# Reordering the first block's projections (values ahead of keys, low parts ahead of modulation sums) and splitting p's projection into three single-pass products

## The reference, cut to what matters

```python
x = layer_norm(x, ln_emb_g, ln_emb_b)
z = x @ w_in[i]
xs, gs, cq, ckv, kr, gm = jnp.split(z, IN_SPLIT_POINTS, axis=-1)
ys = s5_branch(xs, ...) * jax.nn.silu(gs)      # state space branch: y @ w_glu
ym = mla_branch(cq, ckv, kr, ...)              # q = norm(cq) @ w_uq, kv = norm(ckv) @ w_ukv, rotary
...
ple = jax.nn.sigmoid(u @ w_pg[i]) * (p[i] @ w_pp[i])
```

## Time and profile before

| | |
|---|---|
| median of 3 runs | 2211.8 us |
| the profiled execution | 2214.04 us, its span 2211.3 us |
| granted TensorE clock, mean | 0.986 |
| PE busy | 96% |
| DVE, POOL, ACT busy | 56%, 56%, 35% |

### The profile page before, as it was taken

One profiled execution on the slowest core, in us unless ns is written; L12 is line 12 of the kernel. 1 busy time (PEld: TensorE's weight loads), 2 busy tenths in 40 slices (PEclk: granted clock), 3 DMA queues, 4 the chain that ended last, 5 costly groups with the idle time before them and its releaser, 6 DMA issues.

```text
span 2211.3 us, 28169 instructions
## 1 busy us (share of the span) xinstructions
PE 2119.7 (96%) x11208; PEld 1653.5 (75%) x11208; DVE 1230.6 (56%) x1476; ACT 777.4 (35%) x1188; POOL 1239.1 (56%) x826
## 2 busy tenths in 40 slices
PE   8989989999998999999999999998899999999998
PEld 3878835878875885578767788786788888888886
DVE  6999836541768115510168226867766666652424
ACT  6222342340117005620174442145454554431211
POOL 1485812047873663337656754473788888844441
PEclk9999989999998999999999999999999999999999
DMA  7462460042332321001221225323122222154112
GB/s 290 141 145 94 110 214 29 1 164 95 104 100 76 120 77 46 28 29 67 55 47 58 96 108 206 122 76 126 43 82 86 86 86 86 58 191 143 48 39 76
DMA packets 66033, 212.68 MB, mean 96 GB/s; under 512 B 15159, under 2 KB 17511, under 8 KB 64719
## 3 DMA queue, kind: packets, MB, share of 16 engines
q1 hardware_dynamic: 52624, 152.73, 20.7%
q10 hardware_dynamic: 9040, 36.45, 4.5%
q0 software_dynamic: 4240, 21.70, 3.5%
HBM read 162.73 MB, written 46.17 MB: 94 GB/s over the span
## 4 chain that ended last, share of the span: by engine, by line
PE 85%; DVE 6%; ACT 3%; POOL 2%; issue 2%; DMA 1%; SPq 0%; ACTq 0%; DVEq 0%
PE ps L3304 22%; PE ps L2916 17%; PE ps L3423 11%; PE ps L2938 6%; PE ps L3228 4%; PE ps L3337 3%; PE ps L2881 3%; PE ps L3375 2%; PE ps L355 2%; PE ps L525 1%; PE ps L513 1%; PE ps L378 1%; PE ps L1036 1%; PE ps L507 1%; PE ps L538 1%
## 5 line engine op out<-in xcount | busy, mean ns | idle before, releaser
L1589 POOL TENSOR_TENSOR w_parts<-front,sb_zero 128x1024 fp32r<-128x1024 f32 x69 | 140.7, 2039 | 282.1 <-PE ps L3423 117.7
L1664 POOL TENSOR_TENSOR up_parts<-front,up_parts 128x512 fp32r<-128x512 f32 x120 | 194.5, 1628 | 70.4 <-ACT up_parts L1966 70.3
L3423 PE MATMUL ps<-ffn_parts,w_parts 128*128 128x512 f32 x1008 | 230.3, 389 | 1.5 <-DVE front L2842 1.5
L1594 POOL TENSOR_TENSOR w_parts<-front,w_parts 128x1024 fp32r<-128x1024 f32 x75 | 208.5, 2780 | 22.2 <-ACT w_parts L2121 7.5
L3423 PEld LDWEIGHTS ps<-ffn_parts,w_parts 128*128 128x128 f32 x1008 | 189.0, 188 | 41.7 <-issue 2.6
L3304 PE MATMUL ps<-t_high,up_parts 128*128 128x512 f32 x640 | 205.6, 392 | 5.8 <-ACT back L1973 4.6
L2916 PE MATMUL ps<-h_high,w_parts 128*128 128x512 f32 x672 | 187.6, 394 | 0.6 <-PE ps L3228 0.6
L1474 POOL TENSOR_TENSOR front<-front,sb_csilu 128x1024 f32<-128x1024 f32 x48 | 102.2, 2129 | 114.4 <-DMA front<-w_ada 114.4
L3304 PE MATMUL ps<-h_high,up_parts 128*128 128x512 f32 x480 | 154.6, 389 | 1.5 <-DVE back L2610 1.5
L3304 PEld LDWEIGHTS ps<-t_high,up_parts 128*128 128x128 f32 x640 | 121.4, 190 | 31.9 <-issue 6.5
L2916 PEld LDWEIGHTS ps<-h_high,w_parts 128*128 128x128 f32 x672 | 124.0, 188 | 25.8 <-issue 1.4
(11 more groups left out here) (429 smaller groups left out, 4870.8 us busy)
## 6 DMA issues: line engine op xcount, KB each, us to landing
front<-w_ada SPq DMA_DIRECT2D x48, 512.0 KB, 3.7
front<-w_up SPq DMA_DIRECT2D x44, 512.0 KB, 4.4
front<-w_down SPq DMA_DIRECT2D x22, 512.0 KB, 3.5
front<-w_in SPq DMA_DIRECT2D x16, 512.0 KB, 4.8
front<-w_out SPq DMA_DIRECT2D x16, 512.0 KB, 4.9
residual<-back ACTq DMA_DIRECT2D x2, 4096.0 KB, 15.6
front<-w_gates SPq DMA_DIRECT2D x16, 512.0 KB, 4.1
gates<-back SPq DMA_DIRECT2D x16, 512.0 KB, 3.6
```

Source lines behind the costliest of these rows:

```text
L1589: pool.tensor_tensor(high, raw, zero[:, 0:1].to_broadcast((P, PAGE)), ALU.add)\
L1594: pool.tensor_tensor(low, raw, high.bitcast(F32), ALU.subtract).then_inc(S("w_split"), 1)
L1664: pool.tensor_tensor(parts[:, BANK:], src, parts[:, 0:BANK].bitcast(F32), ALU.subtract)\
L3423: mm = pe.matmul(ps[:, 2 * m + nt, :], parts[n % 2 + w_][:, at:at + P], half_of(AR[kk % 4 + x_], nt), start=k == 0 and q == 0, stop=k == N ...
```

## The change

p's projection: p and the first weights come in halves and quarters; they are rounded (weights by ACT, p by DVE) and their low parts made (GpSimd, DVE), and each half becomes six single-pass products. Halves 0 to 7 go by token half; ten halves instead of eight stand ahead of the sums over x. DVE evacuates halves 10, 11 and 12 between centring and the reciprocal, ACT the others. GpSimd makes the low part of a tile's weights ahead of the modulation sum, and PE's column moves from k=0 to k=6 of the tile. The spread for kv moves in front of tile 15's last 16 products, the one for q behind the third round of states. The values come ahead of the keys, the keys use banks 5, 0, 2 and 5, the rotated q and the sigmoid's tiles start in banks 4 to 7. In GpSimd's queue the stores of y come first and the gates' loads last.

```diff
...
-        PP_BANK = (4, 5, 6, 7, 0, 1, 4, 5, 0, 1, 2, 0, 1, 2, 3, 2)
-
-        def pp_half(pe, s):
-
...
+        PP_HALF = [(m, nt) for nt in range(2) for m in range(4)] + [divmod(s, 2) for s in range(8, 16)]
+        PP_BANK = (4, 5, 6, 7, 0, 1, 4, 5, 6, 7, 0, 1, 2, 2, 3, 2)
...
+
...
+
+        def pp_products(pe, halves, ready=None):
+
+            for n, (w_, x_) in enumerate(((W_PP_HIGH, PT_HIGH), (W_PP_LOW, PT_HIGH), (W_PP_HIGH, PT_LOW))):
+                for s in halves:
+                    if ready:
+                        ready(n, s)
+                    m, nt = PP_HALF[s]
+                    for kt in range(2):
+                        at = kt * BANK + m % 4 * P
+                        mm = pe.matmul(ps[:, PP_BANK[s], :], w_[:, m // 4, at:at + P],
+                                       x_[:, kt, nt * BANK:(nt + 1) * BANK], start=n == 0 and kt == 0,
+                                       stop=n == 2 and kt == 1)
+                    if n == 2:
+                        mm.then_inc(S("pp_tile"), 1)
         def embed_pe(pe):
-            pe.wait_ge(S("p_landed"), 32)
...
+            def first_ready(n, s):
+
+                if s == 0 and n != 1:
+                    pe.wait_ge(S("dve_step"), DVE_STEP["p_high0" if n == 0 else "p_low0"])
+                if s in (0, 2) and n == 0:
+                    pe.wait_ge(S("act_step"), ACT_STEP["w_pp_high0"] + s // 2)
+                elif s in (0, 2) and n == 1:
+                    pe.wait_ge(S("pool_step"), POOL_STEP["w_pp_low0"] + s // 2)
+
+            pp_products(pe, (0, 1, 2, 3), first_ready)
+            pe.wait_ge(S("dve_step"), DVE_STEP["p_low1"])
+            pp_products(pe, (4, 5))
+            pe.wait_ge(S("pp_free"), 1)
+            pp_products(pe, (6, 7))
+            pe.wait_ge(S("pp_free"), 2)
+            pe.wait_ge(S("act_step"), ACT_STEP["w_pp_high2"])
+            pe.wait_ge(S("pool_step"), POOL_STEP["w_pp_low2"])
+            pp_products(pe, (8, 9))
             pe.wait_ge(S("x_added"), 1)
...
-            pe.wait_ge(S("pp_free"), 3)
+            pe.wait_ge(S("pp_free"), 5)
             pe.wait_ge(S("norm_stat_read"), 1)
...
-            pe.wait_ge(S("w_pp_landed"), 16)
-            pp_half(pe, 8)
-            pp_half(pe, 9)
+            pp_products(pe, (10, 11))
             for k in range(FT):
-                if k == 2:
-                    pp_half(pe, 10)
+                if k == 3:
+                    pp_products(pe, (12,))
                 pe.wait_ge(S("norm_square"), k + 1)
                 sum_tiles(pe, 3, ones[:], TEMPS_1[k % 2], k == 0, k == FT - 1).then_inc(S("norm_square_used"), 1)
-            pe.wait_ge(S("pp_free"), 4)
-            pp_half(pe, 11)
+            pe.wait_ge(S("pp_read_dve"), 2)
+            pp_products(pe, (13,))
             pe.wait_ge(S("norm_rstd"), 1)
             spread_tiles(pe, TEMPS_1[2][:, 256:512]).then_inc(S("norm_spread"), 1)
-            pp_half(pe, 12)
-            pe.wait_ge(S("pp_free"), 5)
-            pp_half(pe, 13)
-            pe.wait_ge(S("norm_std"), 1)
-            pp_half(pe, 14)
-            pe.wait_ge(S("pp_free"), 8)
-            pp_half(pe, 15)
+            pp_products(pe, (14,))
+            pe.wait_ge(S("pp_free"), 6)
+            pp_products(pe, (15,))
...
+            def projected(s, n=2):
+
+                m, nt = PP_HALF[s]
                 act.wait_ge(S("pp_tile"), s + n)
...
-
-            for m in range(1, 4):
-                projected(2 * m, 2, m)
...
+                if s < 8:
+                    dst, src = PP_FIRST[0][:, m:m + 2, nt * BANK:(nt + 1) * BANK], ps[:, PP_BANK[s]:PP_BANK[s] + 2, :]
+                else:
+                    dst = PP_FIRST[1][:, m % 4, nt * BANK:(nt + n) * BANK]
+                    src = ps[:, PP_BANK[s]:PP_BANK[s] + n, :].rearrange("p a b -> p (a b)")
+                act.activation(dst, src, ACT.Copy).then_inc(S("pp_free"), 1)
+
+            projected(0)
+            act.wait_ge(S("w_pp_landed"), 16)
+            act.activation(pp_piece(W_PP_HIGH, 2), pp_piece(W_PP, 2), ACT.Copy).then_inc(S("act_step"), 1)
+            projected(2)
+            projected(4)
+            projected(6)
+            act.wait_ge(S("pp_free"), 4)
             act.dma_start(pp_dram[0], PP_FIRST[0]).then_inc(S("pp_out0"), 16)
+            projected(8)
             for k in range(FT):
...
                 act.activation(TEMPS_1[k % 2], XN[:, k, :], ACT.Square).then_inc(S("norm_square"), 1)
-            projected(8, 2, 4)
...
-            projected(10, 1, 5)
             in_high(act, 0)
-            projected(11, 1, 6)
+            projected(13, 1)
             in_high(act, 1)
-            late = {0: 12, 2: 13, 3: 14, 5: 15}
             for k in range(FT):
                 act.wait_ge(S("norm_scaled"), k + 1)
                 act.activation(XH[k], XN[:, k, :], ACT.Identity, bias=V("ln_emb_b", k)).then_inc(S("norm_ready"), 1)
-                if k in late:
-                    projected(late[k], 1, 0)
-            act.wait_ge(S("pp_free"), 10)
+            projected(14, 1)
+            projected(15, 1)
+            act.wait_ge(S("pp_free"), 8)
+            act.wait_ge(S("pp_read_dve"), 2)
...
         def embed_dve(dve, link):
-            dve.wait_ge(S("pp_tile"), 2)
-            dve.tensor_copy(PP_FIRST[0][:, 0, :], two(4)).then_inc(S("pp_read_dve"), 1)
             for k in range(1, 6):
...
+            for s, n in ((10, 2), (12, 1)):
+                m, nt = PP_HALF[s]
+                dve.wait_ge(S("pp_tile"), s + n)
+                dve.tensor_copy(PP_FIRST[1][:, m % 4, nt * BANK:(nt + n) * BANK],
+                                ps[:, PP_BANK[s]:PP_BANK[s] + n, :].rearrange("p a b -> p (a b)"))\
+                    .then_inc(S("pp_read_dve"), 1)
...
+        K_BANK = (5, 0, 2, 5)
...
-            sp.dma_start(PT_FIRST, t["pT"].rearrange("(k p) t -> p k t", p=P)).then_inc(S("p_landed"), 16)
-            sp.dma_start(W_PP[:, 0, :], t["w_pp"][0]).then_inc(S("p_landed"), 16)
+            p_in = t["pT"].rearrange("(k p) t -> p k t", p=P)
+            w_pp_in = t["w_pp"][0].rearrange("p (k n) -> p k n", k=2)
+            sp.dma_start(PT_FIRST[:, :, 0:BANK], p_in[:, :, 0:BANK]).then_inc(S("p_landed"), 16)
+            sp.dma_start(pp_piece(W_PP, 0), w_pp_in[:, :, 0:256]).then_inc(S("p_landed"), 16)
+            sp.dma_start(pp_piece(W_PP, 1), w_pp_in[:, :, 256:512]).then_inc(S("p_weight_landed"), 16)
+            sp.dma_start(PT_FIRST[:, :, BANK:2 * BANK], p_in[:, :, BANK:2 * BANK]).then_inc(S("p_later_landed"), 16)
             sp.dma_start(XN[:, 0:2, :], x_in[:, 0:2, :]).then_inc(S("landed0"), 16)
             sp.dma_start(W_PP[:, 1, :], t["w_pp"][1]).then_inc(S("w_pp_landed"), 16)
...
+            for i in range(3):
+                pool.wait_ge(S("act_step"), ACT_STEP[f"w_pp_high{i}"])
+                pool.tensor_tensor(pp_piece(W_PP_LOW, i), pp_piece(W_PP, i), pp_piece(W_PP_HIGH, i).bitcast(F32),
+                                   ALU.subtract).then_inc(S("pool_step"), 1)
...
             for i in range(6, N_IN):
-                ada_sum(i - 4)
...
                 in_low(i)
+                ada_sum(i - 4)
...
-            pool.dma_start(GS, silu_dram[0:4].rearrange("k p t -> p k t")).then_inc(S("silu_back"), 16)
-            pool.dma_start(GM, silu_dram[4:8].rearrange("k p t -> p k t")).then_inc(S("silu_back"), 16)
+            pool.wait_ge(S("ssm_ps_read"), 32)
+            for s in range(STEP):
+                pool.dma_start(y_dram.rearrange("(g c) t -> c g t", c=GC)[:, :, s * CHUNKS:(s + 1) * CHUNKS],
+                               UU[s * GC:(s + 1) * GC, :, :]).then_inc(S("y_in_dram"), 16)
             pool.wait_ge(S("z_free"), N_IN)
             pool.wait_ge(S("dve_step"), DVE_STEP["cm_zero"])
...
             pool.wait_ge(S("y_in_dram"), 16 * STEP)
             pool.dma_start(YF, y_dram.rearrange("(k p) t -> p k t", p=P)).then_inc(S("yf_landed"), 16)
+            pool.wait_ge(S("gate_out0"), 64)
+            pool.wait_ge(S("gate_out1"), 64)
+            pool.wait_ge(S("z_tile"), N_IN)
+            pool.dma_start(GS, silu_dram[0:4].rearrange("k p t -> p k t")).then_inc(S("silu_back"), 16)
+            pool.dma_start(GM, silu_dram[4:8].rearrange("k p t -> p k t")).then_inc(S("silu_back"), 16)
...
+            act.wait_ge(S("p_landed"), 32)
+            act.activation(pp_piece(W_PP_HIGH, 0), pp_piece(W_PP, 0), ACT.Copy).then_inc(S("act_step"), 1)
+            act.wait_ge(S("p_weight_landed"), 16)
+            act.activation(pp_piece(W_PP_HIGH, 1), pp_piece(W_PP, 1), ACT.Copy).then_inc(S("act_step"), 1)
...
-            latent_gain_act(act, 1)
-            latent_gain_act(act, 2)
-
+            for kt in range(8):
+                act.wait_ge(*T("kv_tile", kt + 1))
+                act.activation(VT[:, kt, :], ps[:, kt % 4, :], ACT.Copy).then_inc(S("kv_free"), 1)
+                if kt in (3, 5):
+                    latent_gain_act(act, kt // 2)
             for m in range(4):
...
+                act.wait_ge(*T("kv_tile", 8 + m + 1))
```

(78 more changed lines are left out.)

59 lines of the change are left out of this document (12 added, 47 removed).

## The result

The changed kernel takes 2220.8 us (median of ten runs) against 2213.9 for the kernel before: a ratio of 1.0033, interval [1.0024, 1.0042]. It is slower by 0.33%, where I had forecast 2197.6. The profiled execution has a span of 2219.8 us against 2211.3. At the start of the first attention, where I meant to count, PE is at 376.6 us against 367.9: +8.7 instead of -14.2.

A forecast was written before the change was run, and what follows sets the result against it. TensorE, busy 96% of the span, was taken as the bound; 2.4 kept before V + 12.2 (V first) - 4.6 (q_low stall) + 4.2 (rotated q) = 14.2 us off 2211.8, giving 2197.6, range 2191 to 2206.

The forecast's parts named there:

- the y stores: GpSimd's queue: stores begin at 279.3, last lands at 295.7, rotary loads with or behind them; counted nothing, bound 5.9 us.
- the new wait: PE at q tile 2 waits for q_low behind DVE's rotary: 2.9 us stall plus 1.7 half clock, minus 4.6.
- the old one: Rotated q, in banks 4 to 7, no longer waits for q_low: plus 2.5 and 1.7 of clock, 4.2 us.
- Low parts ahead of sums: Before tile 6, PE's 5.21 us stall and 1.5 us of half clock go: 6.7 us, putting PE 8.3 ahead.
- The spread in the last tile: In tile 15 PE stalls some 4.3 us on DVE's reciprocal ending at 252.65; of 8.3 us PE keeps 2.4.
- rival B: DVE's chain is shorter than thought, PE doesn't stall in tile 15: 8.3 instead of 2.4, 2191.7 us; chance 0.15.
- V ahead of keys: V and keys on PE take 14.4 us instead of 26.6, without the k_low stalls and half clock: gain 12.2.
- p's projection: At the start, PE reaches the sums at 22.3, gain 0.75; DVE's scaling and chain come 1.6 us earlier.
- ScalarE's gain of 1.65: ACT evacuates tile 8 before the squares, so the root ends at 36.65 instead of 38.31, 1.65 us earlier.
- C: Rotary loads land late behind the last store: DVE starts at 301, 5.9 us more stall, 2204.5 us; chance 0.17.
- E: PE stays at half clock after the new stall in tile 15; if from 253 to 303, 2222.6 us; chance 0.06.
- D: Net within measurement: C with DVE's chain no earlier, or slow p's projection; gain 5.3, 2206.5 us; chance 0.12.

The follow-up runs named there:

- GpSimd's DMA order alone: Kernel before with only GpSimd's queue reordered: y stores ahead of the rotary loads, silu loads behind the load of y; ratio 1.0020.
- rotary first: Changed kernel with the rotary loads (and mask) put ahead of the y stores in GpSimd's queue; 2211.5 us, ratio 0.9979.
- Block 10 later: Changed kernel with ScalarE's split of input block 10 moved behind the eight state evacuations; ratio 1.0015.
- sums first: GpSimd's modulation sum again ahead of each low part, PE's columns in their old order: ratio 1.0023 on the changed kernel, 0.9955 on the mended kernel.
- mended kernel: Changed kernel with rotary loads ahead of the y stores, y stores in halves, and ScalarE's split of block 10 later; 2198.5 us, ratio 0.9937.
- the kernel that lets it through: Kernel before with V ahead of the keys, y stores in halves and the silu loads moved to the end of GpSimd's queue; ratio 0.9955.

## Why the prediction was wrong, step by step

**The step that failed** is the y stores: "I count nothing, as DVE comes at 295.1; the bound is 5.9". Both halves are wrong. The stores were to land "11.4 us later", at 295.7; they landed 19.9 us after their last issue, at 311.69. Of these 16.0 us, 7.4 are PE's late arrival (the stores began at 286.70, not 279.3) and 8.5 the longer landing. The rotary loads were to come with them or 5 us behind; they took 17.8 us. I had carried over a landing time from a trace in which less went on beside it. Two parts of the change stretch the whole stores, each by itself (one trace each). With before's order of V and keys and the stores issued ahead of the rotary loads (GpSimd's DMA order alone) they took 18.7 us; with before's DMA order and V first alone, 16.9; with neither, 11.3 to 13.1 in three traces. Why is argued. In before SP's two w_uq blocks were issued from 282.5, ahead of the stores, and w_glu's at 292.3 and 306.3; in after all four fall between 289.1 and 300.1, beside the stores, since V first moves the columns and the keys that free their slots. No run held SP's loads back. That what stands ahead in the queue sets the landing is shown by the two kernels that differ in the silu loads alone, and by the rotary loads on SP's queue.

**A waiter was missing.** I listed who waits behind DVE, not who waits for the stores. ScalarE's q_high does. With this wait alone (rotary first) PE stood 8.3 us for q_low. By my own times q would begin at 292.4, its first q_high be wanted near 296.2 (3.8 us later, as in before) and the stores land at 295.7: the 4.3 us to spare had shrunk to 0.5, on a landing time taken once. The wait was to be seen in the code, and that it had no room left in my own times.

Together: from q's start to that of the rotated q before took 16.4 us; I had 4.6 more for the new wait and 2.5 less for the old one, 18.6. It took 32.6 (301.36 to 333.93). That is 14.0 of the miss of 22.9 us, and w_uq's 1.7, which I had not priced, comes on top.

**Low parts ahead of sums**: right as far as tile 6 (no stall, no half clock), apart from a 1.52 us wait of the first column for its sum at 123.77, which I had put at zero. Wrong in "PE is now 1.6 + 6.7 = 8.3 us ahead": it was 4.7 at tile 6, and nothing of a lead reached tile 15. Of the input blocks I wrote that they "still land before their use": PE's use of them is late, but ScalarE waits for them first, in order, with PE's evacuations behind, and it does so in before's program too. A lead in front of a bound that does not move is lost there; the gathers are the second one, and I had not listed them. Block 10 later gave back 4 us; sums first changed nothing in after and costs some 4 us in the mended kernel.

**The spread in the last tile**: wrong in its reason. The reciprocal whose end I had put at 252.65 started at 244.63, 7.9 us earlier than before, and DVE then waited 16.45 us for PE. DVE's chain was shorter, as rival B had it, though its start did not move. But I took DVE for a chain of fixed length, and it is none: in seven traces with the program of before up to there the reciprocal starts at 247.4 to 254.2, in four with that of the change at 243.3 to 246.6. Earlier it is, by some 5 us. Why stays open: GpSimd was busy 10.7 us of 197 to 220 against 18.8 before, which fits B, but with the sums first again it still starts at 245.87. The 4.3 us stall never came (PE waited only 0.91 us in tile 15, for a modulation sum), and yet the lead that B would have kept was gone already at tile 9.

**V ahead of keys**: right, 14.44 us for 14.4, and 12.1 us in the trace (10 in the ratio) of the kernel that lets it through.

**p's projection**: wrong in both terms. The sums start at 24.28, not 22.3, as 60 products took 16.2 us and not 15.3, and PE waited 0.92 us for the third weight piece. ScalarE's gain of 1.65 did not exist: before, the root started at 37.85, but PE's last sum of squares ended only at 37.73 (37.09 + 0.64), so the evacuation ahead of the root hid. I took the instruction before it on its engine for its cause without looking at its other input.

```profile
15.23 7.07 DVE L1157 TENSOR_TENSOR back<-back,front 128x1024 f32<-128x1024 f32 x4
...
17.96 3.26 POOL L1526 TENSOR_TENSOR w_pp_low<-back,w_pp_high 128x1024 fp32r<-128x1024 f32 x1 [7.36 <-ACT w_pp_high L1128]
```

The four adds took 7.07 us beside GpSimd's subtraction and 5.01 without. The Trainium skill (SBUF — State Buffer, section SBUF: two separate sides) has the loser of the shared port pair block for the whole instruction; the trace agrees with 2.06 of the 2.35 us that I gave for it. They ended at 22.30, before PE was ready, and did not bind.

**The rivals.** C named the place (the rotary waiting for DMA beyond 297 was my own mark for it), with 5.9 us where it was 14.6 on DVE. The Trainium skill (DMA: Bandwidth & Descriptors, section Queues, rings and completion order) says of SP's and ACT's queues that each DMA engine takes its descriptors in ring order. The traces show the like for GpSimd's, with 7.3 us for rotary loads at the head of it and 20.5 behind 4 MB. E did not come from tile 15: the half clock stood behind the 15.26 us wait, and cost 2.7 us there. D's gain is 5.7 us by its own terms (14.2 less C's 6.9 and 1.6), not 5.3, which changes nothing here. The range failed because its ends came from the same row as the value: a transfer taken once, at one load of the queues.

The miss adds up: +4.85 at the end of the states instead of -2.4 (7.3, of which some 2.7 is the luck of before's trace at tile 9, 169.22 against a mean of 171.9), w_uq 1.7, and 14.0 at q_low; V and keys and the rotated q came within 0.2 us of what I had. In the medians the kernel is 6.9 us slower, in the traces 8.7.

## What to carry to other kernels

Before bringing work forward, list every wait of every engine from the new time on, those also that the profile shows at zero: a transfer that lands 4.3 us before its use is a bound as soon as the use moves by more. A landing time belongs to what is queued ahead of it and beside it; when DMAs are reordered, order the queue by when each is needed (here: rotary loads, stores in halves, and 4 MB that nobody waits for at the end) and price the others by it. Ask of every lead which bounds ahead of it do not move; and take the scatter of a single trace (5 us at tile 9 here) before explaining a difference by it. An engine that waits for a load not yet needed passes this wait to all behind it in its queue.

## What the runs showed of the hardware

A 256 KB load from GpSimd's queue took 7.3 us to land at the head of it and 20.5 us behind 4 MB; the same load from SP's queue, beside 2 MB of stores in GpSimd's, took 5.8. Eight stores of 2 MB in all landed 11.3 to 19.9 us after their last issue, and the second half of them 6.8 to 8.3, or 14.8 and 19.7 with the 4 MB of silu loads ahead. I had not expected the half grant to depend on the execution: after the same two stalls for k_low (3.98 and 2.46 us), the 16 records on line 3066 took 8.76 us before, with a grant of 0.50 in 298 to 300 us, and 7.11, at 1.00, in the trace of the kernel that only moved its silu loads. Of the 4.5 us by which that kernel's last stretch was shorter, its ratio of 0.9997 shows nothing.
